# Moving the split weight tiles by 64 and 256 bytes, and the activation tiles onto a 2048-byte grid

## The reference

```python
h = h + _even_mixer(rmsnorm(h), ev_w_in, ev_w_out, ...)    # layer 0: retention and RWKV-7 heads
h = h + square(relu(rmsnorm(h) @ ff_w1[0])) @ ff_w2[0]      # 2048 -> 8192 -> 2048
h = h + _odd_mixer(rmsnorm(h), od_w_in, ..., od_w_out)      # layer 1: conv, gates, linear recurrence
h = h + square(relu(rmsnorm(h) @ ff_w1[1])) @ ff_w2[1]
return rmsnorm(h)
```

## Time and profile before

| | |
|---|---|
| median of 3 runs | 2471.58 us (2471.53 to 2472.12) |
| the profiled execution | 2473.3 us, its span 2471.6 us |
| TensorE, matmuls | busy 2425.5 us, 98%, 11710 of them |
| TensorE, loads of weights | 2024.6 us, 82% |
| VectorE, ScalarE, GpSimd | 57%, 46%, 10% |
| granted TensorE clock | 0.995 |
| DMA | 411 MB, 166 GB/s over the span |

### The profile page before, as it was taken

One profiled execution on the slowest core, in us unless ns is written; L12 is line 12 of the kernel. 1 busy time (PEld: TensorE's weight loads), 2 busy tenths in 40 slices (PEclk: granted clock), 3 DMA queues, 4 the chain that ended last, 5 costly groups with the idle time before them and its releaser, 6 DMA issues.

```text
span 2471.6 us, 32124 instructions
## 1 busy us (share of the span) xinstructions
PE 2425.5 (98%) x11710; PEld 2024.6 (82%) x11710; DVE 1411.0 (57%) x1613; ACT 1132.6 (46%) x1459; POOL 239.2 (10%) x184
## 2 busy tenths in 40 slices
PE   7999999999999999999999999989999999999998
PEld 6878888888888888888888888878888888888886
DVE  5466777776555545445455566775554554454454
ACT  5454444444444344344344445765543443443443
POOL 0001123342000000000000000230000000000001
PEclk9999999999999999999999999999999999999999
DMA  6642232333566565565566565545666656656654
GB/s 217 188 145 87 79 94 79 87 86 104 170 183 186 186 189 185 188 187 186 189 187 186 180 199 168 179 153 180 186 185 190 184 185 190 186 187 188 188 187 153
DMA packets 215432, 411.21 MB, mean 166 GB/s; under 512 B 13264, under 2 KB 19792, under 8 KB 215184
## 3 DMA queue, kind: packets, MB, share of 16 engines
q1 hardware_dynamic: 213888, 407.01, 53.9%
q0 software_dynamic: 1424, 2.49, 0.4%
HBM read 407.35 MB, written 2.10 MB: 166 GB/s over the span
## 4 chain that ended last, share of the span: by engine, by line
PE 88%; DVE 2%; ACT 2%; issue 1%; POOL 0%; ACTq 0%; DVEq 0%; POOLq 0%
PE acc L204 26%; PE acc L206 25%; PE acc L205 25%; PE tp L687 6%; PE tp L301 2%; PE acc L687 1%; PE acc L1489 1%; PE tp L1489 1%; DVE stg L634 0%; ACT w_hi L188 0%; ACT L679 0%; DVE w_lo L193 0%; DVE state L857 0%; DVE gate_t L1552 0%; DVE stg L635 0%
## 5 line engine op out<-in xcount | busy, mean ns | idle before, releaser
L193 DVE TENSOR_TENSOR w_lo<-raw,w_hi 128x1024 fp32r<-128x1024 f32 (+1 forms) x760 | 992.2, 1311 | 908.2 <-ACT w_hi L188 906.6
L188 ACT ACTIVATE w_hi<-raw 128x1024 fp32r<-128x1024 f32 (+1 forms) x760 | 800.4, 1055 | 964.3 <-PE acc L206 957.2
L204 PE MATMUL acc<-w_hi,xT_hi 128*128 128x512 f32 (+1 forms) x1760 | 706.3, 401 | 5.8 <-DVE w_lo L193 4.3
L206 PE MATMUL acc<-w_hi,xT_lo 128*128 128x512 f32 (+1 forms) x1760 | 684.7, 389 | 0.0
L205 PE MATMUL acc<-w_lo,xT_hi 128*128 128x512 f32 (+1 forms) x1760 | 683.9, 389 | 0.0
L204 PEld LDWEIGHTS acc<-w_hi,xT_hi 128*128 128x128 f32 x1760 | 332.1, 189 | 68.5 <-DVE w_lo L193 4.3
L206 PEld LDWEIGHTS acc<-w_hi,xT_lo 128*128 128x128 f32 x1760 | 331.1, 188 | 68.6
L205 PEld LDWEIGHTS acc<-w_lo,xT_hi 128*128 128x128 f32 x1760 | 332.2, 189 | 60.8
L204 PE MATMUL acc<-w_hi,hidA_hi 128*128 128x512 f32 x640 | 256.2, 400 | 6.3 <-DVE hidA_lo L1523 6.3
L205 PE MATMUL acc<-w_lo,hidA_hi 128*128 128x512 f32 x640 | 254.5, 398 | 0.0
L206 PE MATMUL acc<-w_hi,hidA_lo 128*128 128x512 f32 x640 | 254.1, 397 | 0.0
(11 more groups left out here) (230 smaller groups left out, 1728.4 us busy)
## 6 DMA issues: line engine op xcount, KB each, us to landing
raw<-in_ff_w SPq DMA_DIRECT2D x512, 512.0 KB, 3.7
raw<-in_ev_w_in SPq DMA_DIRECT2D x112, 512.0 KB, 3.7
raw<-in_od_w_in SPq DMA_DIRECT2D x64, 512.0 KB, 4.3
raw<-in_ev_w_out SPq DMA_DIRECT2D x32, 512.0 KB, 3.8
raw<-in_od_w_out SPq DMA_DIRECT2D x32, 512.0 KB, 3.8
raw<-in_ev_w_in SPq DMA_DIRECT2D x8, 288.0 KB, 5.8
x<-in_x_in SPq DMA_DIRECT2D x4, 512.0 KB, 6.9
gate_w<-in_gx_w SPq DMA_DIRECT2D x8, 256.0 KB, 2.9
```

Source lines behind the costliest of these rows:

```text
L188: act.activation(w_hi[:, j % RING, :, 0:wide], raw[:, j % RING, :, 0:wide], ACT.Copy).then_inc(hi_ready, 1)
L193: dve.tensor_tensor(w_lo[:, j % RING, :, 0:wide], raw[:, j % RING, :, 0:wide], w_hi[:, j % RING, :, 0:wide], ALU.subtract).then_inc(lo_rea ...
L204: nc.tensor.matmul(o, hi[:, tok], wh, start=(kt == 0), stop=False)
L206: last = nc.tensor.matmul(o, lo[:, tok], wh, start=False, stop=(kt == KT - 1))
```

## The change

The high weight tiles start 64 bytes further along, and the low ones 256 bytes further along (64 + 192). The region shared by the stages starts at the next multiple of 2048 bytes of the slab. The parameters, constants and staging tiles, which lay in front of it, lie behind it now. No instruction is added, removed or put elsewhere.

```diff
         raw = lasting("raw", [P, RING, KU, WIDE])
+        lasting.at += 64
         w_hi = lasting("w_hi", [P, RING, KU, WIDE], F32R)
+        lasting.at += 192
         w_lo = lasting("w_lo", [P, RING, KU, WIDE], F32R)
+        HALF = KT // 2 * T * 4
+        low = -(-lasting.at // 2048) * 2048
+        shared_end = low + 93568
+
+        lasting = Region(shared_end)
         par = lasting("par", [P, NPAR])
...
         ident = con[:, CIDENT:CIDENT + P]
-        HALF = KT // 2 * T * 4
-
-
-        low = lasting.at + -(slab_start + lasting.at) % (2 * P)
+
         at_a = Region(low)
```

## The result

The changed kernel takes 2502.69 us (median of 4 runs, 2501.76 to 2503.15) against 2471.85 us for the kernel before beside it (2471.53 to 2472.25): ratio 1.0124, 95% interval 1.0108 to 1.0139. It is slower by 31 us where a gain of 22 was forecast, and 0.7 us above the end of the stated range. Its profiled execution took 2501.76 us, with a span of 2500.1.

What follows compares the result with a forecast made beforehand. TensorE's pace over its own queue, mostly 9024 fp32r matmuls, was taken as the bound. The hid tiles' gain of 21.9 us, all else 0, gave 2471.6 - 21.9 = 2449.7, rounded to 2450 us; range 2387 to 2502.

Steps and rivals of the forecast that it cites:

- What bounds the kernel, and the handle: TensorE's pace through its own queue, mostly 9024 fp32r matmuls, sets the end; buffer addresses are the change's only handle.
- The hid term: Matmuls with hid tiles, moved from 1408 to 0 past 2048, take xT's pace: 3840 x 5.7 ns, 21.9 us off.
- The shifts: Moving w_hi by 64 and w_lo by 256 bytes costs 0 centrally, bounded by +29.6 us and 118 us off.
- The slow rival: Shifted weight tiles break the fast rhythm with xT, needing one 2048 grid: all matmuls at 232.4 ns, 2501 us; chance 0.34.
- Its variant: Only matmuls reading w_hi lose the fast pace, those reading w_lo keep it: +12.4, 2484 us; within the 0.34.
- The range's end: Upper end of the forecast range, 2502 us, all fp32r matmuls at the slow pace; 0.08 left above.
- The streams taken apart: Shifts keep weight load and moving stream from meeting in memory; w_hi matmuls at 216 ns: 2385 us; chance 0.24.
- No effect of the place: hid's pace has another cause and offsets are not felt: 2471.6 us; chance 0.12, including gain and loss within 0.2%.
- Small tiles and the splits: New residues of par, con, stg, junk and RWKV tiles, and ScalarE's and VectorE's splits hidden under matmuls: 0 each.

Runs made afterwards that it cites:

- the grid alone: Changed kernel with w_hi and w_lo put back on the 2048-byte grid, hid tiles kept on it: 2449.92 us, ratio 0.9911 to the kernel before.
- the map: Kernel with the trunk left out, TensorE alone running the three products at 48 placements of stationary and weight tiles: 226.7 ns a matmul on the 2048-byte grid.
- the bare kernels: Two kernels with the trunk left out, TensorE alone; one varied tile placements, the other also column counts and float32: fp32r 512-column gaps 226.7 ns on the 2048-byte grid.
- (0, 64, 64): Bytes past the 2048-byte grid of stationary tiles, w_hi, w_lo; against the changed kernel, w_lo at 64 instead of 256: 2466.24 us, ratio 0.9978.

## Why the prediction was wrong

*What bounds the kernel, and the handle.* Right. TensorE's pace over 9024 matmuls set the time in every run of the whole kernel: its waits add up to 31.5 to 33.6 us in each of them. And the place of a buffer was what moved it.

*The hid term*, -21.9 us. Right as the part by itself: 22.1 us measured with the grid alone. It was argued from two residues that could have been absolute or relative, and 2048 or anything that divides it. The runs say relative, and 256: the kernel before had hid at 1408, 128 past a multiple of 256, and in the changed kernel it lies at 0, but 64 from the high tiles.

*The shifts*, taken as 0. This is the step that failed: "64 bytes is the smaller part of a row of 2048", and slices that step by 512 and 1024 bytes at one pace, "so steps of these sizes do nothing there; 256 is half of such a step". The row is sound, but it shows only that the pattern's period divides 512. It leaves 256 open, which turned out free (2449.52 us), and says nothing about 64, which is inside the period and costs 51.5 us alone (2501.39 against 2449.92). With the hid gain of 22.1 taken off, 51.5 - 22.1 = 29 us is what this leaves as the loss of the changed kernel, 31 measured. The rest, the 1.3 us between 2501.39 and 2502.69, is within the spread of the two versions' runs.

*The slow rival.* Its size was right, 2501 for 2502.7, with a chance of 0.34. In part that is luck: it used the pace of one offset (128 bytes in the period of 256, 232.4 ns) for another (64 bytes), and the map has prices between 228.9 and 234.4 ns off the grid. Of its mechanism half holds. The fast rhythm does need an alignment between the moving and the stationary tiles, but of 256 bytes, not 2048, and what takes its place is another regular rhythm, 700 ns for three. Its variant, in which only the matmuls that read the displaced tile pay, is wrong: with w_hi alone displaced the gaps with xT after w_lo rose by 5.0 ns (227.4 to 232.4), nearly as much as the 6.8 and 6.0 after w_hi.

*The range's end*, 2502. It rested on 232.4 ns as the slow end, "all at the slow pace", with the remark that a higher time would mean a pace that the trace did not hold. It did hold none: the new one is 233.3 in a locked stretch. One nanosecond over 9024 matmuls is 9 us, more than the 0.7 us by which the range was missed; the short runs between other work in the RWKV part give some of it back: from 340 to 600 us of the kernel before, the gaps after 483 matmuls with xT grew by 0.7 ns each, against 6.1 ns from 1200 to 1600 us. The end should have had room for a worse offset than the only one that the trace showed.

*The streams taken apart* (216 ns). None of the 48 placements with 512 columns came below 226.7. The comparison with float32 was a wrong ground: float32 takes 215.8 ns for 256 columns and 429.2 for 512, nearly twice, 2.5 ns over the 213.3 and 426.7 that two cycles of 2.4 GHz for each column would take, and the 13.3 ns of fp32r are there at 256 columns too. The Trainium skill's figure of N / 2.4 GHz plus about 2.5 ns (page "TensorE: Matmul & The Clock Gate", section "Wait — 56ns, not 53.3ns?") is 215.7 ns for 512 columns. By these runs that is the gap of float32 with 256 columns, 215.8 ns, and no fp32r matmul of 512 columns met it at any placement.

*No effect of the place.* Wrong, by 53 us between the best and the worst whole kernel here (2449.47 and 2502.69). The remark that the move takes hidA_hi alone under byte 131072 was wrong too: with the slab's 16512 bytes, most of hidA_lo goes under it as well. Nothing hangs on it, since distance explains the runs. The Trainium skill, page "SBUF — State Buffer", section "Who interferes with whom", has the moving operand and the weight load on independent read ports and says that PE never waits on anyone. These runs speak against independence where it concerns the two streams of TensorE itself, with one engine running: moving one of the two tiles took the gap from 226.7 to 233.3 ns, and moving both together left it at 226.7. In what it says of the other engines they agree: the pace was the same with ScalarE, VectorE and the DMA at work and without them (226.7, 232.4 and 233.3 ns in the kernels, 226.7, 232.3 and 233.3 in the map).

*Small tiles and the splits*, 0. Right within what can be told: the version that moves hid alone and the one that moves the small tiles as well are 0.3 us apart.

*What stays open* is the mechanism below the pattern: why 256 bytes, why narrower loads do not help, why 384 and 256 columns do not pay for the place, and what the entry changes. The runs exclude other engines and absolute place, and they speak against a collision that grows with the length of the load.

## What to carry to other kernels

Where a kernel is bound by fp32r matmuls of 512 columns, place the stationary and the moving tiles a multiple of 256 bytes from each other, counting both from the same origin; here that was worth 0.9% in one line, and 64 bytes in one tile cost 2.1%. To find out, compare the distance between starts, not durations or busy share, for groups of one shape that differ in their buffer. A pitch at which nothing happens shows only that the period divides it: the price of an offset smaller than every step in the trace is unknown, and its bounds are not those of the one displaced buffer at hand.

## What the runs showed that was not expected

- Every rhythm is an exact pattern. On the grid each matmul takes 226.7 ns, a hid stretch of the kernel before repeats every seven matmuls, in 1626.7 ns, and most of the changed kernel every six, in 1400 ns. In the bare kernels each fp32r placement repeats after 1 to 15 matmuls, and each of these periods is a multiple of 6.67 ns, 16 cycles at 2.4 GHz, to within the trace's 1 ns (34, 244 and 210 of them in the three named). So what looks like wandering in the earlier trace rows is the pattern of seven.
- One placement, (0, 64, 64), can run at 233.3 or 228.9 ns, depending on what ran before it, and holds the one it fell into over 96 matmuls. In the whole kernel it ran at 229 ns, in all ten executions within 2465.8 to 2468.1 us.
- Each fp32r matmul on the grid takes 13.3 ns over its columns at 2.4 GHz, whether it has 512, 384 or 256 of them. A stationary slice of 32 columns 32 bytes off the grid made the gap 240.0 ns, the slowest fp32r gap of all.
